# Joints between projections by token halves, and a rewoven first stage, in a two-block transformer kernel

## The reference

```python
def first_block(x, c, ...):
    c_act = silu(c)
    for l in range(2):
        mod = c_act @ ada_w[l] + ada_b[l]              # 1024 -> 6144: six rows of 1024
        sh_m, sc_m, gt_m, sh_f, sc_f, gt_f = split(mod, 6)
        h = rms_norm(x, norm_mix[l]) * (1 + sc_m) + sh_m
        y = hybrid_mixer(h) if l == 0 else retention_mixer(h)
        x = x + gt_m * y
        h = rms_norm(x, norm_ffn[l]) * (1 + sc_f) + sh_f
        x = x + gt_f * swiglu(h)

def hybrid_mixer(h):
    gq, gk, gv, gate, ga, gb, sq, sk, sv = split(h @ w_in)
    o_a = rms_norm(gated_delta_rule(conv(gq), conv(gk), conv(gv), g, beta)) * silu(gate)
    o_b = stick_breaking_attention(rms_norm(sq), rms_norm(sk), sv)
    return concat(o_a, o_b) @ w_out                    # 512 + 512 -> 1024

def second_block(x, ...):
    for l in range(2):
        mix = concat(rms_norm(y_lru), rms_norm(y_nsa)) @ w_out[l]
        x = layer_norm(ALPHA * x + mix)                # "l1"
        x = layer_norm(ALPHA * x + peer(x))            # "l2": 16384 experts, 128 units each way
```

## Time and profile before

| | |
|---|---|
| median of 3 runs | 3037.66 us (3035.28 to 3038.02) |
| profiled execution: time, span | 3035.38 us, 3033.5 us |
| busy: PE, PEld, DVE, ACT | 94%, 83%, 73%, 52% of the span |
| chain that ended last | PE 75%, DVE 16%, ACT 6%, issue 2%, DMA 1% |
| mean granted TensorE clock | 0.971 of full speed |
| ACT_TABLE_LOAD | 1.283 us each |
| GB/s, first two of 40 slices of 76 us | 268, 138 |
| store of 128 KB (`gs<-xmem`), issue to landing | 3.7 us, median of 248 |

### The profile page before, as it was taken

The page is one execution under the profiler, slowest core; times in us unless marked ns, Lnnn a source line. Parts: engine busy times, 40 slices in busy tenths (PEclk is TensorE's granted clock), DMA queues, the critical chain, the costliest instruction groups (busy, mean ns, idle before and its releaser), DMA issues.

```text
span 3033.5 us, 46635 instructions
## 1 busy us (share of the span) xinstructions
PE 2851.3 (94%) x17894; PEld 2514.8 (83%) x17894; DVE 2221.2 (73%) x3624; ACT 1589.3 (52%) x2726; POOL 87.7 (3%) x150
## 2 busy tenths in 40 slices
PE   7888999999999899899999999999898999999997
PEld 4675798876898877899999888887698999988886
DVE  4654677775554556899898888865589998978887
ACT  2422443334444543477887555535346688855553
POOL 1000001010000200000000000020000000000000
PEclk9998999999999989999999999998899999999999
DMA  7423567584466514566667777762256656687774
GB/s 268 138 84 104 188 247 275 185 282 126 142 185 187 188 57 129 182 203 197 192 195 237 243 241 243 241 209 84 93 179 187 203 192 194 198 264 242 242 241 161
DMA packets 211532, 579.78 MB, mean 191 GB/s; under 512 B 24080, under 2 KB 87856, under 8 KB 210032
## 3 DMA queue, kind: packets, MB, share of 16 engines
q1 hardware_dynamic: 161552, 491.00, 50.8%
q0 software_dynamic: 14048, 53.28, 5.3%
q10 hardware_dynamic: 35712, 32.52, 3.1%
HBM read 541.05 MB, written 35.65 MB: 190 GB/s over the span
## 4 chain that ended last, share of the span: by engine, by line
PE 75%; DVE 16%; ACT 6%; issue 2%; DMA 1%; ACTq 0%; DVEq 0%; POOLq 0%
PE psum L718 73%; DVE wr L1979 4%; DVE gmem L1979 4%; DVE oh_r L1979 3%; ACT gmem L1414 2%; DVE gmem L1982 2%; ACT wr L1414 2%; ACT crf L1414 1%; PE psum L767 1%; DVE xmem L1982 1%; DVE gmem L2781 1%; DVE xr L1979 0%; ACT xmem L1414 0%; ACT L1414 0%; ACTq L1922 0%
## 5 line engine op out<-in xcount | busy, mean ns | idle before, releaser
L1979 DVE TENSOR_TENSOR wr<-raw,wr 128x1024 fp32r<-128x1024 f32 (+1 forms) x814 | 994.2, 1223 | 473.8 <-ACT wr L1414 471.1
L718 PE MATMUL psum<-xr,wr 128*128 128x256 f32 x10464 | 1303.5, 285 | 26.9 <-DVE wr L1979 14.8
L718 PEld LDWEIGHTS psum<-xr,wr 128*128 128x128 f32 x10464 | 1278.3, 193 | 43.3 <-DVE xr L1979 12.8
L1414 ACT ACTIVATE wr<-raw 128x1024 fp32r<-128x1024 f32 (+1 forms) x814 | 853.9, 1049 | 288.8 <-PE psum L718 272.6
L718 PE MATMUL psum<-wr,cr 128*128 128x512 f32 x3072 | 696.8, 389 | 3.0 <-DVE cr L1979 3.0
L718 PEld LDWEIGHTS psum<-wr,cr 128*128 128x128 f32 x3072 | 576.4, 188 | 122.9 <-ACT cr L1414 3.3
L1414 ACT ACTIVATE gmem<-psum 128x512 f32<-128x512 f32 (+2 forms) x309 | 163.3, 540 | 263.0 <-PE psum L718 229.4
L1414 ACT ACTIVATE cr<-xmem 128x256 fp32r<-128x256 f32 x256 | 107.2, 419 | 340.5 <-PE psum L718 338.5
L718 PE MATMUL psum<-wr,xr 128*128 128x512 f32 (+1 forms) x960 | 242.1, 410 | 19.4 <-DVE xr L1979 7.1
L718 PEld LDWEIGHTS psum<-wr,xr 128*128 128x128 f32 x960 | 184.4, 200 | 66.6 <-issue 13.5
L718 PE MATMUL psum<-gmem 128*128 128x128 f32 (+8 forms) x1352 | 194.9, 298 | 11.6 <-DVE gmem L1979 8.7
(11 more groups left out here) (150 smaller groups left out, 1695.2 us busy)
## 6 DMA issues: line engine op xcount, KB each, us to landing
raw<-in_uv SPq DMA_DIRECT2D x512, 512.0 KB, 4.8
raw<-in_ffn_in SPq DMA_DIRECT2D x88, 512.0 KB, 4.1
gs<-xmem ACTq DMA_DIRECT2D x248, 128.0 KB, 3.7
xmem<-gs SPq DMA_DIRECT2D x248, 128.0 KB, 4.4
gmem<-in_ada_w POOLq DMA_DIRECT2D x56, 512.0 KB, 4.3
raw<-in_ffn_out SPq DMA_DIRECT2D x44, 512.0 KB, 3.6
raw<-in_ada_w SPq DMA_DIRECT2D x40, 512.0 KB, 3.6
raw<-in_ret_a SPq DMA_DIRECT2D x32, 512.0 KB, 4.4
```

What stands on the lines that cost most here:

```text
L718: ins = pe.matmul(o, a, b, start=first and i == 0, stop=final and i == len(pairs) - 1, skip_group_check=skip)
L1414: return act.activation(o, a, func, **k)
L1979: return dve.tensor_tensor(o, a, b, op)
```

## The change

1. **Last pair by halves.** `out_last` runs the last two units of each output projection, and of the experts' second products, token half by token half, and signals `half` when tokens 0 to 127 are done. Residual, squares, variance, root and scaling now go half by half behind `half` and the unit's own signal.
2. **Norms.** `ada_norm` computes x times scale before it waits for the root, then h times root plus shift by column halves, each with its own signal. Each half has its own root. `layer_norm` takes the sum into its loop.
3. **Moved.** The split of the next stage's second unit (VectorE), and the zero fills, go behind the norm. ScalarE loads the square root's table in an earlier unit. The fillers of a joint are fewer (4 or 5 matmuls for 7 to 10).
4. **Output.** Two stores of 128 tokens instead of one of 256.
5. **First stage.** Blocks 7 and 9 (ADDED) are multiplied and summed over inputs on VectorE (`ada_acc`), the sum over partitions by one matmul with `ones`; their units alternate with those of blocks 6 and 8. The first two units of SECOND run ahead of `gdn`. `stick` joins behind the second third of `stick_rows`. The four output units of stick's features (k = 4 to 7) run first, with four strand steps behind each; then the last turn and k = 0 to 3.
6. **Start.** POOL's loads wait for unit 15, and VectorE does the low halves of units 16 and 17 behind the last modulation row.

```diff
-    FIRST, SECOND, THIRD = (2, 0, 3, 1), (4, 5), (6, 7, 8, 9)
+    FIRST = [(m, q) for m in (2, 0, 3, 1) for q in range(4)]
+    SECOND = [(m, q) for m in (4, 5) for q in range(4)]
+    THIRD = [(m + i, q) for m in (6, 8) for q in range(4) for i in range(2)]
+    ADDED = (7, 9)
+    HYB_OUT = (4, 5, 6, 7, 0, 1, 2, 3)
...
-        for m in SECOND:
-            for q in range(4):
-                bg.run(2)
-                s["modulate"](m, q)
+        for i, (m, q) in enumerate(SECOND):
+            if i > 1:
+                bg.run(3)
+            s["modulate"](m, q)
+        stick = s["stick"]()
         for c in range(3):
             for i in range(4):
                 s["stick_rows"](c, i)
                 bg.run(3)
-        bg.add(s["stick"]())
-        for m in THIRD:
-            for q in range(4):
-                s["modulate"](m, q)
-                bg.run(4)
+            if c == 1:
+                bg.add(stick)
+        for i, (m, q) in enumerate(THIRD):
+            s["modulate"](m, q)
+            if i % 2:
+                bg.run(6)
+        bg.until_done(stick)
+        s["hybrid_turn"](1)
+        for k in HYB_OUT[0:4]:
+            s["hybrid_out"](k)
+            bg.run(4)
         bg.finish()
-        s["hybrid_turn"]()
-        for k in range(8):
+        s["hybrid_turn"](0)
+        for k in HYB_OUT[4:8]:
             s["hybrid_out"](k)
...
+        def out_last(b, c_of, ks, sig):
+            pair = [(k, *next_unit()) for k in ks]
+            for a in range(2):
+                for k, j, hi, lo in pair:
+                    for n in range(2):
+                        e = slice(512 * n, 512 * n + 512)
+                        ch, cl = c_of(k)
+                        ins = mm3(bank(b + 2 * a + n), [(ch[:, quarter(a)], cl[:, quarter(a)], hi[:, e], lo[:, e])],
+                                  False, k == ks[1], True)
+                    if a:
+                        ins.then_inc(*W.pe.up(j))
+                    elif k == ks[1]:
+                        ins.then_inc(*X.pe.up(("half", sig)))
...
         def ada_norm(tag):             
-            busy(*{("ffn", 0): (7, 9), "ret": (3, 10), ("ffn", 1): (7, 9)}[tag])
+            busy(3 if tag == "ret" else 7, 4)
...
         def modulate(m, q):
-            split()
+            if m == 1 and q > 1:
+                ahead.step()
+            else:
+                split()
+            if m in ADDED:
+                j = ahead.unit
+                dve.wait_ge(raw_in[j % NRAW], 16 * (j // NRAW + 1))
+                for k in range(2):
...
+                    if q + k == 0:
+                        ts(ada_acc, r, c, None, ALU.mult).then_inc(*X.dve.up())
+                    else:
+                        own(X)
+                        stt(ada_acc, r, c, ada_acc, ALU.mult, ALU.add).then_inc(*X.dve.up(("used", j) if k else None))
...
         def ada_norm(tag): 
-            dve.wait_ge(*N.act[tag, "sq", 1])
-            root(N, tag, ss, 1.0 / D, EPS)
-            for a in range(2):
+            for a in range(2):
+                v = ss[:, a:a + 1]
+                dve.wait_ge(*N.act[tag, "sq", a])
+                ts(v, v, 1.0 / D, EPS, ALU.mult, ALU.add).then_inc(*N.dve.up((tag, "var", a)))
+                tt(h[:, a, :], x[:, a, :], aa, ALU.mult).then_inc(*N.dve.up())
+                dve.wait_ge(*N.act[tag, "root", a])
+                dve.reciprocal(v, v).then_inc(*N.dve.up())
                 own(N)
-                stt(h[:, a, :], x[:, a, :], ss[:, a:a + 1], aa, ALU.mult, ALU.mult).then_inc(*N.dve.up())
-                own(N)
-                tt(h[:, a, :], h[:, a, :], sh, ALU.add).then_inc(*N.dve.up((tag, "h", a)))
+                for g in range(2):
+                    e = slice(512 * g, 512 * g + 512)
+                    stt(h[:, a, e], h[:, a, e], v, sh[:, e], ALU.mult, ALU.add).then_inc(*N.dve.up((tag, "h", a, g)))
...
         def peer_v(l, e):              
+            if e == NEXP - 2:
+                pe.wait_ge(*X.dve["c", l, NEXP - 1])
+                out_last(0, lambda k: (ccr[:, k % 2, 0, :], ccr[:, k % 2, 1, :]), (NEXP - 2, NEXP - 1), ("l2", l))
...
-        sp.wait_ge(*N.dve[("l2", 1), "x", 1])
-        sp.dma_start(out.rearrange("(a p) n -> p a n", p=P), x).then_inc(out_sem, 16)
-        sp.wait_ge(out_sem, 16)
+        for a in range(2):
+            sp.wait_ge(*N.dve[("l2", 1), "x", a])
+            sp.dma_start(out[128 * a:128 * a + 128, :], x[:, a, :]).then_inc(out_sem, 16)
+        sp.wait_ge(out_sem, 32)
...
-        pool.wait_ge(*W.pe[9])
+        pool.wait_ge(*W.pe[15])
```

More of the change, by code:

```diff
@@ L268, in program @@
     BACK = list(range(NEXP - 4, NEXP)) + list(range(NEXP - 4))
-    FIRST, SECOND, THIRD = (2, 0, 3, 1), (4, 5), (6, 7, 8, 9)
+    FIRST = [(m, q) for m in (2, 0, 3, 1) for q in range(4)]
+    SECOND = [(m, q) for m in (4, 5) for q in range(4)]
+    THIRD = [(m + i, q) for m in (6, 8) for q in range(4) for i in range(2)]
+    ADDED = (7, 9)
+    added = set()
     def add_plain(blocks):
-        for m in blocks:
-            plain.update(range(len(units), len(units) + 4))
-            units.extend((dr["ada_w"][0, m, q], UNIT) for q in range(4))
+        for m, q in blocks:
+            (added if m in ADDED else plain).add(len(units))
+            units.append((dr["ada_w"][0, m, q], UNIT))
     add_plain(FIRST)
@@ L282, in program @@
     add_plain(THIRD)
-    units += [(dr["hyb_out"][k], UNIT) for k in range(8)]
+    HYB_OUT = (4, 5, 6, 7, 0, 1, 2, 3)
+    units += [(dr["hyb_out"][k], UNIT) for k in HYB_OUT]
     ffn_out = [dr["ffn_out"][l].rearrange("(k p) n -> k p n", p=P) for l in range(2)]
@@ L310, in parts_of @@
         return scaled.get(j, [(0, units[j][1], None)])
-    halved = [j for j in range(NU) if j not in plain]
+    halved = [j for j in range(NU) if j not in plain | added]
     place_of = {j: k for k, j in enumerate(halved)}
@@ L324, in __init__, with step @@
             self.unit, self.next = -1, 0
+        def step(self):
+            self.unit += 1
         def to_split(self, step=1):
@@ L329, in to_split @@
                 self.next += 1
-                if self.next - 1 not in plain:
+                if self.next - 1 not in plain | added:
                     yield self.next - 1
@@ L2342, in stick, with hybrid_turn @@
             yield
-        def hybrid_turn():
+        def hybrid_turn(g):
             for a in range(2):
-                for g in range(2):
-                    lo_of("hyo", xr, a, g, 4 + 2 * a + g)
+                lo_of("hyo", xr, a, g, 2 + a if g else 4 + a)
+            if g:
+                return
             dve.wait_ge(rows_in, 16)
@@ L2350, in hybrid_turn, with residual @@
             stt(top(2), top(2), 1.0, nf0, ALU.add, ALU.mult).then_inc(*X.dve.up())
-        def residual(name, gt, tmp, p_done):
-            dve.wait_ge(*p_done)
+        def residual(name, gt, tmp):
+            ahead.step()
             for a in range(2):
+                dve.wait_ge(*(done() if a else X.pe["half", name]))
                 for n in range(2):
@@ L2365, in hybrid_out @@
         def hybrid_out(k):
-            split()
-            if k == 7:
-                residual("hyb out", top(0), hy_tmp, done())
+            if k == 3:
+                residual("hyb out", top(0), hy_tmp)
+            else:
+                split()
         def mods(part):
@@ L2408, in ffn_out_ @@
         def ffn_out_(l, k):
-            split()
-            if k == FM - 1:
+            if k < FM - 1:
+                split()
+            else:
                 dve.wait_ge(*A.act["row", 13 if l else 1])
-                residual(("ffn out", l), top(3 if l == 0 else 9), ff_h, done())
+                residual(("ffn out", l), top(3 if l == 0 else 9), ff_h)
         def ret_qk(p, i):
@@ L2474, in ret_out_ @@
         def ret_out_(k):
-            split()
-            if k == 15:
-                residual("ret out", top(6), re_tmp, done())
+            if k < 15:
+                split()
+            else:
+                residual("ret out", top(6), re_tmp)
         def mix_start(l):
@@ L2651, in mix_out @@
         def mix_out(l, k):
-            split()
-            if k == 7:
-                dve.wait_ge(*done())
-                dve.wait_ge(*S.dve[("on", l), "rstd"])
-                for i in range(4):
-                    a = i // 2
-                    v = my[:, a, 512 * (i % 2):512 * (i % 2) + 512]
-                    stt(v, bank(2 + i), rn[:, 2 + a:3 + a], v, ALU.mult, ALU.add).then_inc(*X.dve.up(("mix out", l, i)))
+            if k < 7:
+                split()
         def layer_norm(tag, src, g, b_, split_):
@@ L2896, in load @@
             if j >= NRAW:
[L2897 removed]
+                k = j - NRAW
+                sp.wait_ge(*(X.dve["used", k] if k in added else (W.pe if k in plain else W.dve)[k]))
             src, n = units[j]
```

151 lines of the change are left out of this document (101 added, 50 removed).

## The result

The changed kernel takes 2988.11 us (median of 4 runs, 2984.8 to 2991.16) against 3037.84 us before (4 runs): the ratio is 0.9838, 95% interval 0.9821 to 0.9855. Forecast were 2985.0 and a gain of 52.7 us; the gain is 49.7. The profiled execution took 2989.63 us with a span of 2987.8, 45.7 less than the span before: the medians lie 4.0 us further apart than these two traces.

The account below looks back on a forecast made before the run. Bound by a chain, three quarters TensorE and a sixth VectorE. Gains 30.4 (joints and end) + 9.3 + 3.7 + 12 - 2.7 = 52.7 us gave 2985.0 us; range 2980 to 2991 (chance 0.42).

Parts of the forecast that it names:

- Start: First stage's start: POOL's loads moved behind unit 15, projection's first matmul at 45.1 instead of 54.39 us: gain 9.3 us.
- the two units of SECOND: Two modulation units run ahead of the first strand step, in a TensorE wait of 4.73 us: gain 3.7 us.
- A: Weave gives nothing: prologue and added sums push chains, 2 for 12; or loads delay projection, 4 for 9.3; chance 0.22.
- Joints: Between stages: TensorE's waits shrink as VectorE's chain runs by halves; three `ada_norm` 18.5, `mix_start` 4.1, `layer_norm` 4.0 and 2.1 us.
- The end's 1.7: Behind the last matmul: VectorE's chain 10.2 instead of 11.2 us (1.0), last store of half size 0.7.
- Table load: ScalarE's table preload fits an output unit at 1.28 us; by the skill's 2.66, sum some 3 us higher.
- Delta rule and stick: First stage: 14.5 us less TensorE work, 2.5 us more idle, gain 12 us; bounds 2 and 22.
- Clock: Behind joints TensorE's granted clock falls with fewer fillers, 0.5 us at four joints; with the pairs' waits 2.7 us off.
- rival B: Clock falls to 1.2 GHz in each joint and into the next stage, 1.7 us at eight places, 14 us; chance 0.1.
- C: Output and early modulation units fill TensorE's idle in the first stage, 22 for 12: 2975 us; chance 0.18.
- D: Halves come too late because the pair is late: 2.7 us at eight places, 22 us, 3007; chance 0.04.
- E: Slower: VectorE waits for loads of each added unit, strand work queued behind; eight times, 61 us: 3046; chance 0.04.

Follow-up runs that it names:

- the repeat: The changed kernel run once more, unchanged: 2985.86 us, ratio 0.9827 to the kernel before.

## Why the prediction was right, and where not

**Start: right.** Units 12 to 15 without a wait, VectorE at 39.28 (said 39.2), projection at 44.82 (said 45.1). Moving POOL's loads back costs 9.3 us. Where they now run they delay nothing: from the projection to `stick_rows` TensorE waits for no load, its waits for VectorE's splits are 3.5 us as before, and the two units of SECOND still gave their 3.7 us. So the second half of A (4 for 9.3) is out.

**Joints: right, 3 us too small.** `ada_norm` came out at 11.0, 11.4 and 11.0 for 11.7. The laid-out queue ended the second half's norm at 9.05 and it ended at 317.19 - 308.61 = 8.6; low halves 11.6, measured 11.0. The `layer_norm` joints behind a projection were 12.7 and 12.0 for 12.3, and the one behind the expert sum 11.7 with a wait of 1.03 ahead of the pair, 12.7 for 12.9 (the forecast's 1.1 for that wait was a slip: 3013.42 less 3012.5 is 0.9). The end's 1.7 were 2.7, of it 1.3 for 0.7 from the smaller store: the 3.7 us of the small stores were no floor for it. The kernel without the early half shows that this signal carries the joints: without it the median is 30 us longer (3016.1 against 2985.9, two sets).

**Table load: the row decides.** The Trainium skill, page "ScalarE: Activation LUTs", section "What ACT_TABLE_LOAD costs", adds a drain to the load, 2.66 us in all. The trace of the kernel without preloads does not agree: it has 1.28 us with none, and TensorE's wait grows by 1.41. That kernel's median (2994.35) would have fitted the larger figure; no row accounts for it.

**Delta rule and stick: the term that was mis-sized.** 14.5 us less work minus 2.5 more idle was to give 12. The traces give 12.3 less busy time and 7.4 more idle, 4.9, and the joint begins at 308.61 where 302 was named as a sign. The work is as forecast: 32.9 us of matmuls on `raw` became 15.3, and 3.1 for the sums, 14.5 less; other matmuls took 2.2 us more. Of the idle forecast, 26.3 us, the prologue was to be 8 (it is 4.7, by stick's earlier start), the groups 10 (9.2: the 12.8 of the row without the 2.9 ahead of the stage's first unit and 0.7 in the delta rule), the first turn 1.8 (1.8), the delta rule's end 2.5 (0.9), its norm and the second turn 4 (5.2). What the sum put at nothing is a wait of TensorE for its own helper: ahead of `mm(ones, ada_acc)` it waits for VectorE's last accumulation, 2.52 and 4.28 us. And the groups would have fallen to 4.6 us without the added operations, which make two of their waits 1.7 and 2.9 longer. VectorE's sixteen operations took 11.5 us (14 of 0.75, two of 0.48) for 10.5. With `ADDED` empty the stage is 2.9 us shorter: of the change's edits this one costs, as it was placed. Its ledger, from the kernel with and without it: 13.9 us of TensorE's work saved, 3.1 for the sums, 6.8 for the waits on them, 4.6 on the strand's chains, 2.4 for a lower clock, together 3.0 lost. The stage's other edits, output units in the delta rule's end (3 to 5) and stick earlier (about 3), gave what the stage gained. Rival A was nearest here, by the half of it that had the added work push the chains; its other half, the prologue, is out.

**Luck.** This one term was 7 us too large, and 47 us of gain, where rival A begins, lay 5.7 below the forecast. That the time still fell into the forecast is partly luck: the joints gave 3 us more, and the medians lie 4 us further apart than the two traces. By these traces alone the gain is 45.7 us, outside the 47 to 58; in the repeat it is 50.1.

**Clock: in sign, not size.** -2.7 was taken, -3.2 and -5.8 measured. It is not rival B: behind the first joint the clock is 1.00. Of the loss, 1.6 us are behind the second joint in both traces; the rest lies in other stretches in each. The kernel without fillers shows B's price as real: 22.8 us by the medians of the two sets, at seven places, where B put 14 at eight.

**C, D and E** did not occur: output units hid only part of the idle; the pair had its operands, but for 1.03 us behind each expert sum; no row of VectorE waits for `raw` in THIRD.

## What to carry over

When work moves from the bound engine to a free one, price the way back: who waits for the result, how long after it was issued, and what the shortened engine does in the time. Here 13.9 us of matmuls became 11.4 us of waits, 3.1 of summing and a lower clock, and 5.2 us of the waits went when the sum was merely asked for six steps later. Signal a consumer as soon as its first half is whole, for that is worth the half's whole run time or more at each joint (2.7 to 4.1 us here); and put fillers only on a bank that nobody holds.

## What the hardware showed

- A wait can cost twice. With 4.32 instead of 1.67 us of idle time ahead of them, behind the same 3.59 us of fillers, the same eight transposes took 1.97 instead of 1.32 us; a 1.28 us table load made one joint 2.4 us longer and another 1.5. It need not: in the kernel before, 3.49 us of idle time behind 8.74 us of fillers left them at 1.10 us (at 553.84).
- Moving matmuls away slowed ones that stayed: the stage's granted clock was 0.90 to 0.93 in six traces with two blocks on VectorE and 0.94 or 0.95 in three without, and one piece of 28 matmuls, behind a wait of 2.5 instead of 0.8 us, took 5.4 us against 3.81.
- The same stage of the same program took 174.1 to 178.3 us in six executions with idle time alike within 1 us: the rest is granted clock.
- The last store, 128 rows of the output (512 KB) instead of 256, ended 3.06 us behind VectorE instead of 4.4.
